# One unused 512-column product ahead of four stretches of 256-column products, in a two-block transformer kernel on one core

## The reference

```python
def swiglu(h, w_gu, w_down):
    g, u = jnp.split(h @ w_gu, 2, axis=-1)
    return (jax.nn.silu(g) * u) @ w_down

for i in range(DEPTH):                       # first block, DEPTH = 2
    f = swiglu(rms_norm(h, ln_ffn1[i, 0]), ffn1_w_gu[i], ffn1_w_down[i])
    h = h + 0.5 * rms_norm(f, ln_ffn1[i, 1])
    ...                                      # the mixer of this layer
    f = swiglu(rms_norm(h, ln_ffn2[i, 0]), ffn2_w_gu[i], ffn2_w_down[i])
    h = h + 0.5 * rms_norm(f, ln_ffn2[i, 1])

# second block
merged = (jax.nn.sigmoid(gate_a) * (o_a @ w_br_dsa[l]) + jax.nn.sigmoid(gate_b) * (o_b @ w_br_moba[l]))
x = x + gt_m * (merged @ w_out[l])
h = rms_norm_2(x, g_ffn_norm[l]) * (1.0 + sc_f) + sh_f
g_ff, u_ff = jnp.split(h @ w_gate_up[l], 2, axis=-1)
x = x + gt_f * ((jax.nn.silu(g_ff) * u_ff) @ w_down[l])
```

## Time and profile before

| | |
|---|---|
| median of 3 runs | 1469.18 us (1468.82 to 1470.86) |
| profiled execution, span | 1468.2 us |
| TensorE matmul busy | 1446.1 us, 98% |
| TensorE weight load busy | 1406.6 us, 96% |
| VectorE busy | 1056.6 us, 72% |
| ScalarE busy | 700.0 us, 48% |
| HBM read | 266.73 MB |

### The profile page before, as it was taken

How to read it: one execution, slowest core, us unless ns; L and a number is a source line. 1 busy time by engine, 2 the same in 40 slices (tenths; PEclk the granted TensorE clock), 3 DMA queues, 4 the chain that set the end, 5 groups by cost and what they waited for, 6 DMA issues and landing times. The chain is left out here.

```text
span 1468.2 us, 28465 instructions
## 1 busy us (share of the span) xinstructions
PE 1446.1 (98%) x11585; PEld 1406.6 (96%) x11585; DVE 1056.6 (72%) x1439; ACT 700.0 (48%) x910; POOL 29.0 (2%) x58
## 2 busy tenths in 40 slices
PE   8999999999999999999999999999999999999999
PEld 8999999999999999999999889999987899999999
DVE  6766779777667786677878768767887777876652
ACT  6544353454443454443554655443436766544431
POOL 0000100000001000001000000001000000000000
PEclk9999999999999999999999999999999999999999
DMA  9555835437447644458343226647633436365540
GB/s 324 220 187 186 268 149 201 172 106 267 172 172 249 239 173 172 171 196 288 128 173 124 78 70 246 227 173 268 234 115 135 145 139 231 131 228 185 184 173 30
DMA packets 42538, 269.09 MB, mean 183 GB/s; under 512 B 4768, under 2 KB 5920, under 8 KB 13520
## 3 DMA queue, kind: packets, MB, share of 16 engines
q1 hardware_dynamic: 33984, 240.31, 45.1%
q0 software_dynamic: 7312, 26.44, 5.5%
q10 hardware_dynamic: 1152, 1.05, 0.2%
HBM read 266.73 MB, written 1.05 MB: 182 GB/s over the span
## 5 line engine op out<-in xcount | busy, mean ns | idle before, releaser
L418 PE MATMUL ps<-x_hi,w_hi 128*128 128x272 f32 (+2 forms) x2296 | 661.8, 288 | 6.7 <-DVE x_lo L1447 1.9
L420 PE MATMUL ps<-x_hi,w_lo 128*128 128x272 f32 (+2 forms) x2296 | 651.8, 284 | 0.0
L419 PE MATMUL ps<-x_lo,w_hi 128*128 128x272 f32 (+2 forms) x2296 | 651.7, 284 | 0.0
L2024 ACT ACTIVATE w_hi<-raw_weights 128x2048 fp32r<-128x2048 f32 x219 | 416.9, 1912 | 291.6 <-PE ps L420 289.0
L1174 DVE TENSOR_TENSOR w_lo<-raw_weights,w_hi 128x2048 fp32r<-128x2048 f32 x193 | 439.7, 2288 | 143.8 <-ACT w_hi L2024 143.3
L418 PEld LDWEIGHTS ps<-x_hi,w_hi 128*128 128x128 f32 x2296 | 433.1, 189 | 10.8 <-DVE x_lo L1380 2.5
L419 PEld LDWEIGHTS ps<-x_lo,w_hi 128*128 128x128 f32 x2296 | 433.3, 189 | 0.7
L420 PEld LDWEIGHTS ps<-x_hi,w_lo 128*128 128x128 f32 x2296 | 433.1, 189 | 0.0
L418 PE MATMUL ps<-a_hi,w_hi 128*128 128x272 f32 x592 | 169.6, 286 | 0.0
L419 PE MATMUL ps<-a_lo,w_hi 128*128 128x272 f32 x592 | 169.6, 286 | 0.0
L420 PE MATMUL ps<-a_hi,w_lo 128*128 128x272 f32 x592 | 169.6, 286 | 0.0
(11 more groups left out here) (259 smaller groups left out, 1543.9 us busy)
## 6 DMA issues: line engine op xcount, KB each, us to landing
raw_weights<-w_units SPq DMA_DIRECT2D x226, 1024.0 KB, 4.9
mod_w<-mod_units POOLq DMA_DIRECT2D x48, 512.0 KB, 5.5
raw_weights<-w_units SPq DMA_DIRECT2D x4, 256.0 KB, 5.8
raw_weights<-w_units SPq DMA_DIRECT2D x2, 512.0 KB, 9.2
out<-h ACTq DMA_DIRECT2D x8, 128.0 KB, 1.9
h<-x_in SPq DMA_DIRECT2D x2, 272.0 KB, 4.1
h<-x_in SPq DMA_DIRECT2D x1, 544.0 KB, 8.0
tab<-tables POOLq DMA_DIRECT2D x1, 512.0 KB, 7.9
```

The source lines that it names most:

```text
L418: pe.matmul(dst, wh, hi, start=start, stop=False)
L419: pe.matmul(dst, wh, lo, start=False, stop=False)
L420: return pe.matmul(dst, wl, hi, start=False, stop=stop)
L2024: act.activation(w_hi[:, u % RING, :], raw[:, u % RING, :], ACT.Copy).then_inc(S["hi_ready"], 1)
```

## The change

An extra MATMUL with 512 columns is issued at four places. It takes 128 columns of `w_hi` of the unit at hand and two tiles of 256 tokens of the stage's hi activations, and writes a PSUM bank with `start=True`. The next product into that bank is also a `start=True` product and overwrites it, so its result is used nowhere. In down 3, w_out and down 4 it stands in the first unit, ahead of tile 7 (after 21 products of the stage). In up 3 it stands ahead of the loop, after groups 0 and 1 (192 products), behind the two waits that the loop's first products have anyway. Up 4 has none.

```diff
-            def k_outer(st, xs, a_base, done=(), done_units=0, busy=None):
+            def k_outer(st, xs, a_base, done=(), done_units=0, busy=None, long_at=None):
...
                             wait_bank(st, st.t0 + m)
                             if busy is not None and m in busy:
                                 busy[m]()
+                            if m == long_at:
+                                long_product(st.bank(st.t0 + m), u, xs[0])
                         ins = three_pass(ps[:, st.bank(st.t0 + m), 0:st.T], u % RING, (kk * 8 + m) * P,
...
+            def long_product(bank, u, x):
+
+                pe.matmul(ps[:, bank, :].rearrange("p (a n) -> p a n", a=2), w_hi[:, u % RING, 0:P], x[:, 0:2, 0:SEQ],
+                          start=True, stop=True)
...
                 first_groups(st, x_base, part)
+                if n == 3:
+                    pe.wait_ge(S["lo_ready"], st.u0 + 5)
+                    wait_bank(st, st.tile(2))
+                    long_product(st.bank(st.tile(2)), st.u0 + 4, x_hi)
                 with pe.Fori(0, 4) as i:
...
-            k_outer(stages["down", 3], a_of[SEQ], A0["up", 3])
+            k_outer(stages["down", 3], a_of[SEQ], A0["up", 3], long_at=7)
...
-            k_outer(stages["w_out"], (z_hi, z_lo), A0["br"])
+            k_outer(stages["w_out"], (z_hi, z_lo), A0["br"], long_at=7)
             gate_up(4, X0["up", 4])
-            k_outer(stages["down", 4], a_of[SEQ], A0["up", 4])
+            k_outer(stages["down", 4], a_of[SEQ], A0["up", 4], long_at=7)
```

## The result

The changed kernel takes 1473.81 us (median of 19 runs, 1471.74 to 1476.92), the kernel before 1468.82 us (19 runs beside them, 1465.08 to 1473.86). The ratio is 1.0030, with a 95% interval of 1.0021 to 1.0039: slower by 0.30%, some 4.4 us by the ratio (the two medians differ by 5.0). The forecast was 1467.1 us, 0.14% less, within what can't be told from no change. None of the 19 runs of the changed kernel took less than 1471.7 us, while the kernel before goes down to 1465.1.

What follows compares the result with a forecast made beforehand. TensorE's distance between product starts was taken as the bound. Gains of 0.52 us (w_out) and 2.03 (down 4), less 0.51 lost in up 3 and down 3, gave -2.04 us: 1467.1 us, 8-in-10 range 1465.6 to 1470.3.

Steps and rivals of the forecast that it cites:

- The two paces: TensorE's 256-column products start 113.3 or 117.8 ns apart; an interruption settles which, and it is then kept.
- What follows a 512-column product: Behind each inserted product, five distances of 0.12 us, then the 113 ns pace, as behind line 1051's 512-column products.
- this hold-up: In down 3 a product was held up, distances 0.24 and 0.22 us; the seven behind took 0.113 us each.
- Up 3 and down 3 already run at 113.3 ns, each pays 0.25 us: Nothing to gain in up 3 and down 3; their two inserted products lose 0.51 us together.
- rival 2: New product unsettles a good stretch: up 3 loses 3.9 us, down 3 2.3 us; 1471.0 or 1473.3 us; chance 0.11.
- The gains in w_out (0.52) and down 4 (2.03): Products behind the new one, 171 in w_out and 507 in down 4, each gain 4.5 ns, less the product's cost.
- The map from span to run time: The median of the runs was taken to lie 1.0 us above the profiled span of 1468.2 us.
- Up 4: No new product there; its 258-column products were expected to stay 120.8 ns apart behind line 564, with no gain.
- The price of one product: At each of the four places an inserted 512-column product pushes everything behind it by 0.228 us; bounds 0.113 and 0.24.
- The cover at up 4's first group: With w_out 0.5 us earlier, up 4's fourth tile could wait for h_ready; 0.2 us counts against 1.2 us of room.
- The price by the Trainium skill's distance of N/2.4 + 2.5 ns: By the page, 109.2 ns for 256 columns, no pace to win; four products of 215.8 ns cost 0.86 us: about 1470.0.
- the likeliest case: The forecast itself, 1467.1 us for the whole kernel, chance 0.58, with its own range 1466.3 to 1467.9 us.

Runs made afterwards that it cites:

- the second profile: The changed kernel profiled once more without any edit, read for its paces alone: one run, 1471.42 us.
- down 3 alone: Against the changed kernel, the extra 512-column product kept only in down 3, ahead of tile 7: ratio 1.0003 to the kernel before; its profiled run 1474.61 us.
- two 192-column products: Against the kernel before, two 192-column products one position apart, in up 3 and down 4 only: ratio 1.0006; its profiled run 1472.06 us.
- the kernel before again: The kernel before profiled a second time without any edit, read for its paces alone: one run, 1473.75 us; span 1471.7 us.

## Why the prediction was wrong

**The two paces** were read rightly: 113.3 and 117.8 ns, chosen at an interruption and kept. The runs add that one 512-column product is such an interruption every time that it meets the short pace, and 11 times of 15 when it meets the long one.

**The step that failed is "What follows a 512-column product": "I take the short pace."** From the short pace it ends in the long one, 16 times of 16. The earlier trace rows did show products settling at 113 ns behind 512 columns, but behind a stream of them, not behind one that breaks into a short-paced stretch. The earlier trace rows were called the nearest thing, but this hold-up left the short pace standing in five profiles of seven and ended it in two, so its one row was one draw and says little about a product. Against the long pace, which w_out and down 4 had in the earlier trace rows, the short one is indeed the likelier outcome, 11 of 15.

**"Up 3 and down 3 already run at 113.3 ns, each pays 0.25 us"** fell with it: up 3 paid 0.23 + 3.84 us. That was rival 2, whose price was right (3.9 us). Down 3 was returned to the short pace by its own product, in this profile and from a pace that up 3 had spoilt.

**The gains in w_out (0.52) and down 4 (2.03)** needed the long pace to arrive and the right position in it. In the profile of the change both came short and were made long. In the second profile w_out came long and stayed so, and down 4 came short.

**One profile was taken for every execution.** The earlier trace rows have up 3 short, w_out and down 4 long. Of the 14 profiles of this study, up 3 came to its loop short in 8 and long in 6, w_out short in 3 and long in 11, and down 4 short in 7 (one not counted). The three runs before, 2 us apart, were put down to noise; a down stage at the other pace is worth 2.3 us. The map from span to run time was off as well: this study's runs lie 2.1 us above their spans, not 1.0.

**Up 4** did as forecast, 120.8 and 120.9 ns. **The price of one product** was right. The cover at up 4's first group held: no wait appeared. The price by the Trainium skill's distance of N/2.4 + 2.5 ns (TensorE: Matmul & The Clock Gate, Back-to-back issue gap), 0.86 us for the four, has the right sign and too small a size for the whole. That section calls it the gap of an isolated matmul and says that in a stream of weight loads and matmuls both set the spacing; the prediction left this out. No run here shows its 109.2 ns for 256 columns. The second statement fits the long pace, in which one load of three takes 192 ns, but that the load sets the pace is not shown.

**Two slips in its sums** change nothing above. Up 4's group 0 is given 119.2 ns in one place and 120.0 in another; start to start it is 120.0, and the window's count is a little off at its edges. And the bounds of the likeliest case add up to 1467.5 us above, not 1467.9.

**Does the mechanism give the measured size?** Taking the arrivals of the 14 profiles and the tally (4 of 15 stay long), a 512-column product raises up 3's chance of the long pace from 0.43 to 0.57 + 0.43 x 0.27 = 0.69, worth 0.26 x 3.89 = 1.0 us; down 3's, from 0.43 to 0.31 + 0.69 x 0.27 = 0.50, 0.2 us; down 4's from 0.46 to 0.66, 0.5 us; w_out's falls from 0.79 to 0.42, -0.3 us. The product's own time is four times 0.23, 0.9 us. The sum is 2.3 us, below the 3.1 to 5.7 us measured. The times of the runs without a profile narrow it. The three profiled executions in which up 3 and down 3 ran long throughout (down 3 alone, two 192-column products, the kernel before again) took 1474.61, 1472.06 and 1473.75 us; the first profile of the kernel before, with both short, has a span of 1468.2, some 1470.3 us. Of the 83 timed runs of the kernel before, in four sets, 22 took more than 1471 us, and some of these may have down 3 alone long. So up 3 seems to arrive short in 3 of 4 or more, an estimate. With 3 of 4 the sum is about 3.6 us, and with the hold-up of down 3 counted (2 of 7 end long, with and without the change) about 3.1, at the lower end of the interval. So the cause is shown; its full size comes out only roughly.

## What to carry to other kernels

Where TensorE streams back to back, count products per microsecond stage by stage: here two stretches of the same shape that differed by 4% showed two ways for weight loads and products to interleave, and each profile was one draw of them. An unused instruction put in to shift such a lock is a blind throw; look at what it does from both paces, since here it broke the good one every time and mended the bad one in 11 cases of 15. Profile the same kernel twice before attributing a few microseconds to an edit.

## What was not expected of the hardware

- Products of 256 float32r columns with their own 128-column weight load hold either 113.3 or 117.8 ns at the same granted clock of 1.00, for more than 1460 products in a row (the kernel before again, 890 to 1062 us), and find one of them anew after an interruption. What keeps them in one is open. In the booked times it is 276 ns or 281 ns a product, and in the long pace every third weight load is 192 ns in place of 188.
- From the short pace one extra product of 64, 128, 320 or 512 columns ended in the long one (30 cases of 30), one of 192, 256, 288, 384 or 448 left it. Why these widths is open.
- Two more columns (258) cost 7.5 ns a product against the short pace, 120.8 ns, and no interruption tried brought them below some 120.
